# Mixture-of-experts rows in full blocks of 128 and small blocks of at most 64, results stored from ScalarE's queue

## The reference

```
xt = h.reshape(T, D)                                     # T = 512
grp = argmax(group_logits); top_val, top_idx = lax.top_k(in_group, 2)
expert_id = grp * 8 + top_idx                            # 1024 assignments to 32 experts
order = argsort(e_flat); counts = bincount; dest = padded_starts[e] + rank
def expert_block(xb, e):
    return (silu(xb @ w_gate[e]) * (xb @ w_up[e])) @ w_down[e]
out = zeros.at[slot_tok].add(ys * slot_gate)
```

## Time and profile before

| | us |
|---|---|
| median of three runs | 2288.25 (2285.98 to 2289.89) |
| the profiled execution | 2286.19 |
| its span | 2284.6 |
| TensorE matmuls busy | 2112.0 (92%) |
| VectorE busy | 1376.1 (60%) |
| ScalarE busy | 1080.1 (47%) |

### The profile page before, as it was taken

One profiled execution on the slowest core, in us unless ns is written; L12 is line 12 of the kernel. 1 busy time (PEld: TensorE's weight loads), 2 busy tenths in 40 slices (PEclk: granted clock), 3 DMA queues, 4 the chain that ended last, 5 costly groups with the idle time before them and its releaser, 6 DMA issues. The chain is left out here.

```text
span 2284.6 us, 27948 instructions
## 1 busy us (share of the span) xinstructions
PE 2112.0 (92%) x10050; PEld 1705.8 (75%) x10050; DVE 1376.1 (60%) x1775; ACT 1080.1 (47%) x1183; POOL 173.2 (8%) x238
## 2 busy tenths in 40 slices
PE   7999899999998999699999997999878999999993
PEld 5777678888886777488888885777457888888882
DVE  3542247555436455655555436887246899898994
ACT  3335524343322455514343323364325888878883
POOL 2000110000001000100000000000011111111111
PEclk9999999999998999699999998999979999999997
DMA  8232027742322221224332332310128999999994
GB/s 225 66 87 80 19 74 282 217 109 74 129 74 82 86 65 65 74 55 121 92 108 78 116 87 65 93 57 18 42 92 315 414 410 415 410 413 412 411 392 184
DMA packets 223575, 377.38 MB, mean 165 GB/s; under 512 B 12604, under 2 KB 174716, under 8 KB 201080
## 3 DMA queue, kind: packets, MB, share of 16 engines
q1 hardware_dynamic: 206280, 315.21, 39.8%
q0 software_dynamic: 17200, 60.89, 7.2%
HBM read 339.84 MB, written 38.84 MB: 166 GB/s over the span
## 5 line engine op out<-in xcount | busy, mean ns | idle before, releaser
L1004 PE MATMUL PS<-XS,split 128*128 128x512 f32 (+1 forms) x2304 | 482.3, 372 | 3.6 <-DVE XS L154 3.1
L1004 PEld LDWEIGHTS PS<-XS,split 128*128 128x128 f32 x2304 | 406.4, 188 | 79.2 <-DVE XS L154 3.6
L154 DVE TENSOR_TENSOR moe_split<-moe_raw,moe_split 128x2048 fp32r<-128x2048 f32 x174 | 397.1, 2289 | 62.0 <-ACT moe_split L149 59.8
L154 DVE TENSOR_TENSOR split<-ring,split 128x2048 fp32r<-128x2048 f32 x110 | 251.8, 2292 | 275.2 <-ACT split L149 275.0
L2578 PE MATMUL PS<-moe_split,moe_x 128*128 128x512 f32 x1392 | 339.7, 396 | 4.8 <-DVE moe_split L154 4.8
L149 ACT CAST moe_split<-moe_raw 128x2048 fp32r<-128x2048 f32 x174 | 332.6, 1912 | 23.9 <-DMA moe_raw<-in_expert_w_gate 14.4
L149 ACT CAST split<-ring 128x2048 fp32r<-128x2048 f32 x112 | 213.2, 1905 | 207.0 <-PE PS L1040 118.3
L2578 PEld LDWEIGHTS PS<-moe_split,moe_x 128*128 128x128 f32 x1392 | 259.1, 190 | 57.5 <-DVE moe_split L154 5.2
L2600 PE MATMUL PS<-moe_split,moe_h 128*128 128x512 f32 x696 | 164.7, 393 | 2.1 <-DVE moe_h L154 2.1
L2600 PEld LDWEIGHTS PS<-moe_split,moe_h 128*128 128x128 f32 x696 | 130.7, 189 | 31.4 <-DVE moe_h L154 2.2
L1040 PE MATMUL PS<-split,XS 128*128 128x512 f32 x672 | 152.6, 389 | 0.0
(11 more groups left out here) (352 smaller groups left out, 2543.4 us busy)
## 6 DMA issues: line engine op xcount, KB each, us to landing
moe_raw<-in_expert_w_gate SPq DMA_DIRECT2D x58, 1024.0 KB, 7.3
moe_raw<-in_expert_w_up SPq DMA_DIRECT2D x58, 1024.0 KB, 8.2
moe_raw<-in_expert_w_down SPq DMA_DIRECT2D x58, 1024.0 KB, 7.4
ring<-in_w_up SPq DMA_DIRECT2D x88, 512.0 KB, 5.2
ring<-in_w_down SPq DMA_DIRECT2D x44, 512.0 KB, 4.4
expert_rows<-rows POOLq DMA_DIRECT2D x4, 4096.0 KB, 30.1
expert_rows<-W POOLq DMA_DIRECT2D x29, 512.0 KB, 8.4
ring<-in_w_in SPq DMA_DIRECT2D x24, 512.0 KB, 5.3
```

Source lines behind the costliest of these rows:

```text
L154: return dve.tensor_tensor(lo, raw, hi.bitcast(F32), ALU.subtract)
L1004: mm = pe.matmul(PS[:, b + q, rows], w[:, c, q, :], x_half(k, high)[:, c, rows], start=(c == 0 and m == 0), stop=(c == KC - 1 and m == 2))
```

## The change

Each expert's rows are cut into full blocks of 128 and at most one small block of up to 64: a remainder of 65 to 128 makes a full block, one of 1 to 64 a small one. All full blocks come first (at least 3), then all small ones (at least 3). For the counts above that is 7 full and 22 small blocks; before it is 29 of one kind.

- *Routing*: the tables of block numbers are 64 wide (32 full, 32 small). The expert of each block is now summed with the block number on the partition, put on a diagonal and turned to a row by one TensorE matmul, which stands between the counting and the ranking matmuls behind `wait_ge(listed)`.
- *Small blocks*: `small_x` holds low and high halves of 64 rows side by side, so one matmul with 128 stationary columns does low x high and high x high, and one with 64 does high x low: 8 matmuls per product. The low row and the high row sums stand on partitions 64 apart; ScalarE copies gate and up sums to SBUF, TensorE multiplies them by a pair matrix (`turn_small`), which adds the two and transposes. Silu, multiplication and split happen on the turned 256 columns. `down` keeps its 24 matmuls with 64 rows.
- *Results* are saved by ScalarE's own DMA queue; GpSimd only gathers, 64 rows in small blocks.
- `clear_stage` clears all of `expert_rows`, in five DMAs.

```diff
-        for n in range(8, YB, 8):
+        for n in range(0, YB, 8):
...
         mm.then_inc(s.counted, 1)
+        pe.wait_ge(s.listed, 1)
+        pe.matmul(PS[:, 7, 192:192 + NB], k.negone, diagonal, start=True, stop=True).then_inc(s.tabled, 1)
         for t in range(NT):
...
+        full, small = nblk[:, 0:32], nblk[:, 32:64]
+        dve.tensor_scalar(full, cnt, 64.5, None, ALU.is_gt)
...
+        for least, part in ((3.0, full), (3.0, small)):
+            if part is small:
+                dve.scalar_tensor_tensor(small, full, -128.0, cnt, ALU.mult, ALU.add)
+                dve.drain()
+                dve.tensor_scalar(small, small, 0.5, None, ALU.is_gt)
+                dve.drain()
+            dve.tensor_reduce(more, part, AX.X, ALU.add)
+            dve.drain()
+            dve.tensor_scalar(more, more, -1.0, least, ALU.mult, ALU.add)
+            dve.drain()
+            dve.scalar_tensor_tensor(part[:, 31:32], more, 0.0, part[:, 31:32], ALU.max, ALU.add)
+            dve.drain()
         dve.tensor_tensor_scan(ends, nblk, nblk, 0.0, ALU.add, ALU.bypass)
...
-        dve.tensor_tensor(cmpb.rearrange("p (b e) -> p b e", e=32), across(ends, NB), along(slot_iota[:, 0:NB], 32),
-                          ALU.is_le)
+        dve.tensor_scalar(at_block, ends, tokf[:, 0:1], None, ALU.is_le)
+        dve.drain()
+        dve.tensor_reduce(where, at_block, AX.X, ALU.add)
...
+        dve.tensor_scalar(diagonal, k.ident[:, 0:NB], where, None, ALU.mult).then_inc(s.listed, 1)
...
         dve.wait_ge(s.ranked, 1)
-        dve.tensor_tensor(dest, PS[:, 5, 0:128].rearrange("p (t n) -> p t n", t=NT), across(first, NT), ALU.add)
+        rank = PS[:, 5, 0:128].rearrange("p (t n) -> p t n", t=NT)
+        dve.tensor_tensor(dest, rank, across(first[:, 0:32], NT), ALU.add)
+        dve.tensor_tensor(work, rank, across(big128, NT), ALU.is_ge)
+        dve.drain()
+        dve.tensor_tensor(work, work, across(shift, NT), ALU.mult)
+        dve.drain()
+        dve.tensor_tensor(dest, dest, work, ALU.add)
...
+        def small_product(i, m, bank, slot):
+            pe.wait_ge(w_low[m], i + 1)
...
+            for c in range(4):
+                at = 4 * half + c
+                pe.matmul(PS[:, bank, :], k.moe_x[:, 0, at * P:(at + 1) * P], wh[:, c, :],
+                          start=(at == 0), stop=(at == KC - 1), skip_group_check=True)
+                mm = pe.matmul(PS[0:64, bank, :], small_x[:, at, 1, :], wl[:, c, :],
+                               start=False, stop=(at == KC - 1), skip_group_check=True)
+            mm.then_inc(s.used, 1)
+
+        def turn_small(i):
+            pe.wait_ge(s.mids, i + 1)
+            pe.wait_ge(s.ml_out, i + 1)
+            for part, columns in ((0, gate_columns), (1, mid_columns)):
+                for c in range(4):
+                    at = 256 * part + 64 * c
+                    mm = pe.matmul(PS[:, 4, at:at + 64], columns[:, :, c], pair, start=True, stop=True)
+            mm.then_inc(s.mid_turned, 1)
...
+        def save(i, rows=P):
+            act.wait_ge(s.y_kept, i + 2)
+            act.dma_start(y_rows[bass.ds(i * P, rows), :], ys[0:rows, :]).then_inc(s.y_saved, 16)
...
+        def small_body(i, before):
+            small_gate(i)
+            high(i, U)
+            high(i, U + 1)
+            keep(i - 1, rows=before)
+            high(i + 1, G)
+            save(i - 1, before)
+            leave_small(i + 1, 0)
+            high(i + 1, G + 1)
+            small_up(i)
+            leave_small(i + 1, 1)
+            high(i, DN)
+            small_silu(i)
+            high(i, DN + 1)
...
+        def small_mid(i):
+            dve.wait_ge(s.mh_out, i + 1)
+            dve.wait_ge(s.used, place(i - 1, DN + 1) + 1)
+            dve.tensor_tensor(mid_T, PS[:, 4, 256:512], silu_T, ALU.mult)
+            dve.drain()
+            middle = mid_T.rearrange("p (c n) -> p c n", c=4)
+            dve.tensor_copy(midT[1][:, :, 0:64], middle)
+            dve.drain()
+            split_low(dve, middle, midT[1][:, :, 0:64], midT[0][:, :, 0:64]).then_inc(s.ml_out, 1)
```

## The result

The changed kernel takes 2330.8 us (median of 4 runs, 2325.7 to 2333.41) against 2289.07 (4 runs, 2285.98 to 2293.85): ratio 1.0179, 95% interval 1.0161 to 1.0197. It is slower by 1.8%; the forecast was 2278 us, 0.4% faster. The profiled executions are 2333.41 and 2286.19 us, their spans 2331.7 and 2284.6: 47.1 us to explain.

The account below looks back on a forecast made before the run. The prediction took TensorE's stream and a ScalarE-VectorE-`down` ring as tied at 17.80 us a block, DMA close behind. Loop -11.8, routing +5.2 and end -3.5 sum to -10.1 us: forecast 2278 us, range 2264 to 2291.

Parts of the forecast that it names:

- turning the middle 8 instead of 4 (at most 0.9): TensorE in a small block: eight turning operations of the middle instead of four, at most 0.9 us together.
- two passes of 0.25: Routing stage: the table's matmul on the diagonal, priced as two handovers and two passes of 0.25 us, until 1700.8.
- The 14.1 to 14.6 us of TensorE's block: TensorE's summed work in a small block: products 7.3, `down` 5.46, turning x 0.9, turning the middle at most 0.9.
- the ring: Expert loop's cycle through ScalarE, VectorE and `down`: 17.27 us per small block against 17.80 before; loop gain 11.8 us.
- rival (c): TensorE's clock falls because of idle gaps: 10 us more per affected block, two blocks 2298, five 2328; chance 0.08.
- `small_mid`: VectorE in a small block: three drained operations of 256 columns replace one split, 1.47 us with handover against 0.87.
- the mixed block: Period from full to small blocks: the full block's multiply stays, leaves are halved, 0.7 us gained.
- the save at nothing: ScalarE's queue takes the save of results: its issue hides behind the running cast and costs 0.
- rival (a): 64-row transfers load only half the ports or engines, so the loop gains nothing: 2290 us; chance 0.12.
- the clearing: Clearing one more 4 MiB of `expert_rows` beside the first layer's feed-forward: cost 0, bound 10 us of DMA time.
- Routing: Before the loop: TensorE's new wait delays ranks (+4.9 us), first rows come 5.8 later, loop start +5.2.
- The end: Last block and after: -2.0 before `down`, -0.7 within it, -0.8 behind it, together -3.5 us (-1 to -5).

Follow-up runs that it names:

- experiment 1: Changed kernel with the small blocks' turn as eight one-record transposes, low x high sums left out: 2275.11 us, ratio 0.9938.
- experiment 4: Changed kernel with gate and up sums and pair matrix written as fp32r, one record per turning matmul: 2276.8 us, ratio 0.9926.
- experiment 2: Changed kernel with the gate half of the turn done right after product U, ahead of the turn of x: 2299.73 us, ratio 1.0040.
- experiment 6: Changed kernel with the ranking matmuls ahead of the wait for the list and the table's matmul: 2326.44 us, ratio 1.0159.
- experiment 3: Kernel before with its four transposes of the middle as plain float32 matmuls with the identity: 2317.96 us, ratio 1.0111.
- experiment 7: Changed kernel with four idle matmuls before product G: 2329.88 us; between the turn's halves instead: 2330.62. Kernel before with its turn as eight plain matmuls: 2384.39.

## Why the prediction was wrong

- **The step that failed: "turning the middle 8 instead of 4 (at most 0.9)."** It names no row; 0.9 is what eight transposes of x take (0.89 in the earlier trace rows), while the new turn is made of plain float32 matmuls. They measure 3.72, four times the bound, since each leaves two records of 0.23 where a transpose takes 0.14. A row for the form was at hand: the ranking matmuls of the routing are plain float32, and in the earlier trace rows the last three of them (L2318 for t = 3) stand as x6 with 1.47 us, two records each, 0.25 a record at 32 columns. The forecast itself priced the table's matmul so ("two passes of 0.25"); for eight matmuls that is 16 x 0.25 = 4.0. The 14.1 to 14.6 us of TensorE's block become 18.97 - 1.04 = 17.9.
- **It followed that the turn was left off the ring.** The walk of 17.27 has no TensorE between `down` and `down`. With 0.9 that was right: experiments 1 and 4 run at 17.31, with the turn at 1.1 and 1.8. The check that was missing is a second walk, through keep, cast G, low G, leave, product G, a turn of length T, silu, `small_mid` and `down`: with the durations measured now 0.91 + 1.93 + 2.21 + 0.47 + 1.97 + T + 0.53 + 1.35 + 5.85 = 15.2 + T. It takes over from the first ring at T = 2.1. Cost: 21 x (18.97 - 17.31) = 35 us.
- **Clock, rival (c), 0.08.** The clock fell, but neither as given nor for that reason: eleven blocks at 1.33 us (14.6 in all) instead of two to five at 10, and behind the turn, not for the pauses, which experiment 1 has with the clock at 1.00. That (c)'s times, 2298 to 2328, lie nearest to the measured one is luck: 35 of the 47 us are the turn on the ring.
- **Right:** the ring (17.27 forecast, 17.31 without the long turn), `small_mid` (1.47 forecast, 1.35), the mixed block (-0.7 forecast, -0.5), the save at nothing (0.06 to 0.08 a block), 64-row transfers within the ring (rival (a) gone), the clearing: in eight kernels that clear all of `expert_rows` the copy of the counts starts at 1692.6 to 1694.6, as before's at 1694.59. The +4.3 us of the changed kernel's profiled execution lies ahead of every changed routing instruction and came in one other (experiment 2, 1698.70) of nine, so it is put down to scatter between executions; what scatters is open.
- **Routing:** ranks +4.7 (forecast +4.9), first rows +5.6 (forecast +5.8). At the first keep only +3.2 of it is left (forecast 5.2): the gather was no longer waited for, and product U of block 0 took 4.51 us instead of the 5.49 of the earlier trace rows, with a stretch at 0.50 of 3.41 us around it instead of 6.83.
- **The end:** the last period is 2.1 longer instead of 2.7 shorter, with turn and clock again on the path; in experiment 1 it was 1.7 shorter.

## What to carry to other kernels

Price a new operation by a row of its own form: in these traces a transpose (0.14), an fp32r matmul (0.23) and a plain float32 matmul (two records, 0.46) with 64 to 128 moving columns are three prices, and fewer columns did not make them cheaper. When a saving leaves a ring with 0.1 us of room, walk every other cycle through the block with the new durations, and ask at which duration each takes over. When an operation is moved off a ring, look at what is queued behind its new place (experiment 2), and what can be queued before a wait should not stand behind it (experiment 6).

## What the runs showed of the hardware

A plain float32 matmul with 128 stationary columns leaves two records, in rows of eight 0.21 us apart at 64 and at 128 columns; an fp32r one leaves one, 0.21 apart at 64 (experiments 2 to 4). A transpose of 128x128 takes 0.14 (experiment 1). Behind some of the rows of sixteen such float32 records (3.72 us) the granted clock is 0.50 for 3.41 us, in the kernel before even though TensorE never pauses; behind two rows of eight in a block it is not (experiment 7). DMA moved 395 GB/s with 64-row gathers and stores beside the loads (experiment 1).
